# Attention inside a one-core diffusion step: key maxima beside the visits, and softmax sums without GpSimd

## The reference

```
keys = jnp.concatenate([_apply_rope(ak, cos, sin), cache['k']], axis=1)
vals = jnp.concatenate([av, cache['v']], axis=1)
...
s = jnp.einsum('bqkgd,bskd->bkgqs', qblk, k).astype(jnp.float32) * scale
p = jax.nn.softmax(s, axis=-1).astype(v.dtype)
return jnp.einsum('bkgqs,bskd->bqkgd', p, v)
```

## Time and profile before

| | us |
|---|---|
| median of 3 runs | 2387.59 (2383.01 to 2388.78) |
| the profiled execution, its own time | 2383.17 |
| its span, first to last instruction | 2381.4 |
| one steady attention tile (1216.14 to 1247.42) | 31.28 |
| the first attention tile (1156.38 to 1184.86) | 28.48 |
| the last one, to the next stage's first product (1372.62 to 1404.32) | 31.70 |

### The profile page before, as it was taken

How to read it: one execution, slowest core, us unless ns; L and a number is a source line. 1 busy time by engine, 2 the same in 40 slices (tenths; PEclk the granted TensorE clock), 3 DMA queues, 4 the chain that set the end, 5 groups by cost and what they waited for, 6 DMA issues and landing times. The chain is left out here.

```text
span 2381.4 us, 42995 instructions
## 1 busy us (share of the span) xinstructions
PE 2280.1 (96%) x17607; PEld 2024.0 (85%) x17607; DVE 1421.0 (60%) x2180; ACT 803.7 (34%) x1398; POOL 336.4 (14%) x291
## 2 busy tenths in 40 slices
PE   6999999999999999999888889998999999999997
PEld 5887779999999889998655569877999999998886
DVE  5331266533554566765666646768676676667877
ACT  5321132213333223324333444324223223234444
POOL 0000000001110001112466531000121121120001
PEclk9999999999999999999999989999999999999999
DMA  6325623235442533214101128421232232259434
GB/s 278 120 84 184 228 104 116 91 135 202 167 161 96 188 116 107 71 48 164 34 19 64 39 85 327 158 89 68 74 109 91 73 109 91 73 174 274 126 104 124
DMA packets 126875, 295.56 MB, mean 124 GB/s; under 512 B 19808, under 2 KB 63280, under 8 KB 117376
## 3 DMA queue, kind: packets, MB, share of 16 engines
q1 hardware_dynamic: 98112, 238.67, 29.8%
q10 hardware_dynamic: 24640, 39.46, 4.5%
q0 software_dynamic: 3968, 15.21, 1.7%
HBM read 207.83 MB, written 85.53 MB: 123 GB/s over the span
## 5 line engine op out<-in xcount | busy, mean ns | idle before, releaser
L62 PE MATMUL ps<-prj_w,h_hi 128*128 128x512 f32 (+1 forms) x864 | 254.9, 379 | 4.1 <-DVE h_lo L755 4.1
L62 PE MATMUL ps<-h_hi,fill_whi 128*128 128x384 f32 x672 | 235.2, 350 | 4.9 <-ACT fill_st L1119 2.4
L62 PE MATMUL ps<-wt 128*128 128x320 f32 (+2 forms) x1046 | 227.2, 327 | 2.3 <-DVE merged L3315 1.3
L62 PE MATMUL ps<-h_lo,fill_whi 128*128 128x384 f32 x672 | 226.1, 336 | 2.7 <-issue 2.7
L62 PE MATMUL ps<-h_hi,fill_wlo 128*128 128x384 f32 x672 | 226.5, 337 | 0.0
L62 PE MATMUL ps<-ys,mergedr 128*128 128x256 f32 (+1 forms) x1056 | 219.2, 296 | 0.4 <-issue 0.4
L62 PE MATMUL ps<-zb,mergedr 128*128 128x320 f32 (+2 forms) x764 | 200.4, 327 | 4.9 <-issue 2.7
L62 PE MATMUL ps<-zb,wt 128*128 128x384 f32 (+3 forms) x758 | 200.2, 325 | 0.0
L62 PEld LDWEIGHTS ps<-prj_w,h_hi 128*128 128x128 f32 x864 | 158.0, 190 | 42.7 <-issue 10.6
L62 PEld LDWEIGHTS ps<-wt 128*128 128x128 f32 x1046 | 179.6, 189 | 16.7 <-issue 2.6
L62 PEld LDWEIGHTS ps<-ys,mergedr 128*128 128x128 f32 x1056 | 174.2, 190 | 0.7 <-issue 0.7
(11 more groups left out here) (509 smaller groups left out, 4723.1 us busy)
## 6 DMA issues: line engine op xcount, KB each, us to landing
wraw<-in_w_ffn_in SPq DMA_DIRECT2D x22, 1024.0 KB, 5.2
prj_raw<-in_w_ada SPq DMA_DIRECT2D x16, 1024.0 KB, 5.8
fill_raw<-in_w_fill SPq DMA_DIRECT2D x30, 512.0 KB, 4.6
wtf<-a_dram SPq DMA_DIRECT2D x55, 256.0 KB, 2.6
bg_dram<-fill_st ACTq DMA_DIRECT2D x72, 192.0 KB, 2.0
xf<-bg_dram POOLq DMA_DIRECT2D x24, 576.0 KB, 7.1
tok_dram<-prj_tst ACTq DMA_DIRECT2D x45, 256.0 KB, 2.0
prj_raw<-in_w_tok SPq DMA_DIRECT2D x10, 1024.0 KB, 7.0
```

The lines of the kernel that those rows point to most:

```text
L62: mm = pe.matmul(out, lhs[a], rhs[b], start=first and n == 0, stop=last and n == 2, skip_group_check=onto)
```

## The change

Four edits of `attention`; nothing else is touched.

1. `shift` writes the maximum negated in one instruction, straight into `qpart`. The buffer `mx` and the semaphore `nm` are gone.
2. `add_trio` is gone. `sums(n)` multiplies each of the three tiles of a trio by ones: 24 products where there were 8 (the very last trio had 24 already). A ring slot is free when the trio's `sums` is done.
3. TensorE's order within a tile is new: two visits stand back to back and a head after them, `values` is followed at once by the same trio's `sums` (before, the third trio's `sums` fell into the next tile), `shifts(i, 1)` opens the tile, and `queries(i+2, 0)` is done at the end of tile i.
4. VectorE's `next_split(i+1, 1)` comes after head 0, `next_split(i+2, 0)` after head 6, `norm_b` after head 1. ScalarE's list and `turn` follow suit.

```diff
-        turn = lambda i, k: 4 * i + k + (1 if 4 * i + k >= 2 else 0)
+        def turn(i, k):
+            if i == 0:
+                return (0, 1, 3, 5)[k]
+            return 4 * i + (0, 2, 3, 5 if i < LAST else 4)[k]
...
             for i in range(LAST + 1):
-                if i:
-                    add_trio(3 * i - 1)
                 if i + 2 <= LAST:
                     rope(i + 2, 0)
-                add_trio(3 * i)
-                if i + 2 <= LAST:
                     rope(i + 2, 1)
-                add_trio(3 * i + 1)
...
+                if kv == 0 and i >= 3:
+                    pe.wait_ge(sem["norm"], i - 2)
                 turn_queries(pe, kv, PT).then_inc(sem["ptm"], 1)
...
             def shifts(i, kv):
-                pe.wait_ge(sem["nm"], AH * i + G * kv + G)
+                pe.wait_ge(sem["mx"], AH * i + G * kv + G)
                 pe.wait_ge(sem["pte"], turn(i, 2 + kv))
-                if kv == 1 and i >= 2:
+                if kv == 1 and i == LAST:
                     pe.wait_ge(sem["norm"], i - 1)
...
                 i, g = divmod(n, NT // TRIO)
                 if g == 0 and i:
                     pe.wait_ge(sem["rc"], i)
-                if n < LASTG:
-                    pe.wait_ge(sem["paired"], 2 * n + 2)
-                    mm = add(pt[(TRIO * n + TRIO - 1) % RING], g == 0, g == 2)
-                else:
-                    for x in range(TRIO):
-                        mm = add(pt[(TRIO * n + x) % RING], False, x == TRIO - 1)
+                for x in range(TRIO):
+                    mm = add(pt[(TRIO * n + x) % RING], g == 0 and x == 0, g == 2 and x == TRIO - 1)
...
+                shifts(i, 1)
+                head(0)
+                step(0)
+                step(1)
+                head(1)
+                if more:
+                    queries(i + 1, 1)
+                step(2)
+                step(3)
+                head(2)
+                values(i, 0)
+                sums(3 * i)
+                head(3)
+                step(4)
+                step(5)
+                head(4)
+                if more:
+                    shifts(i + 1, 0)
+                step(6)
+                head(5)
+                if i:
+                    spread_sums(i - 1)
+                values(i, 1)
+                sums(3 * i + 1)
+                head(6)
+                step(7)
+                step(8)
+                head(7)
+                if i + 2 <= LAST:
+                    queries(i + 2, 0)
+                values(i, 2)
+                sums(3 * i + 2)
...
-            shifts(0, 1)
+            queries(1, 0)
             for i in range(LAST + 1):
                 tile(i)
...
             def exponentials(i, j):
                 n = NT * i + j
-                b, r = divmod(n - RING, TRIO)
-                if b >= 0 and r < 2:
-                    act.wait_ge(sem["paired"], 2 * b + r + 1)
-                if b >= 0 and r == 2:
-                    act.wait_ge(sem["sums"], b + 1)
+                if n >= RING:
+                    act.wait_ge(sem["sums"], (n - RING) // TRIO + 1)
...
-            shifts(0, 1)
             put(23)
+            queries(1, 0)
...
-                v.tensor_reduce(mx[:, a % 2:a % 2 + 1], ps[:, 0:3, 0:TH], AX.XY, ALU.max).then_inc(sem["mx"], 1)
-                v.wait_ge(sem["mx"], AH * i + h + 1)
-                v.tensor_scalar(qpart[kv][:, a, 0:1], mx[:, a % 2:a % 2 + 1], -1.0, None, ALU.mult).then_inc(sem["nm"], 1)
+                v.tensor_reduce(qpart[kv][:, a, 0:1], ps[:, 0:3, 0:TH], AX.XY, ALU.max, negate=True).then_inc(sem["mx"], 1)
...
-                if 0 <= i < NT - 3:
-                    norm_b(i + 3)
                 for h in range(AH):
                     if i < LAST:
                         shift(i + 1, h)
+                    if 0 <= i < LAST and h == 0:
+                        next_split(i + 1, 1)
+                    if 0 <= i < NT - 3 and h == 1:
+                        norm_b(i + 3)
...
-                if i + 2 <= LAST:
-                    next_split(i + 2, 0)
-                    next_split(i + 2, 1)
+                    if i + 2 <= LAST and h == 6:
+                        next_split(i + 2, 0)
```

More of the change, by code:

```diff
@@ L1891, in attention @@
     RING, TRIO = 6, 3
-    LASTG = (LAT // P) * NT // TRIO - 1
     LAST = LAT // P - 1
@@ L1920, in attention @@
         prc = g.hole
-        mx = ph.sb("mx", [P, 2])
         ones, spread = ph.sb("ones", [P, 32]), ph.sb("spread", [P, G, HD])
@@ L1928, in attention @@
         names = ("load qload const knd kpow kout ktm kte qd qpow rope cpart qtm qte csmm cmx cex cptm cpte comm cdone "
-                 "part s1 mx nm ptm pte s2 ex pv paired sums rc spread norm evict yout0 yout1 kv dve mly mlw mlhi b0y1 b0y2 b0w b0yh b0wh b0yl b0wl b0mm b0ev b0out0 b0out1 b0out2 b0out3 b0out4 b0out5 b1lo")
+                 "part s1 mx ptm pte s2 ex pv sums rc spread norm evict yout0 yout1 kv dve mly mlw mlhi b0y1 b0y2 b0w b0yh b0wh b0yl b0wl b0mm b0ev b0out0 b0out1 b0out2 b0out3 b0out4 b0out5 b1lo")
         sem = {n: ph.sem(n) for n in names.split()}
@@ L2023, in rope @@
                 gp.wait_ge(sem["rope"], 6 * n + 3 * e + 3)
[L2025 to L2031, removed]
             inverse_norm(0)
@@ L2208, in spread_sums @@
                 if i < LAST:
-                    pe.wait_ge(sem["pte"], turn(i + 2, 2) + 1 if i + 2 <= LAST else turn(LAST, 3) + 1)
+                    pe.wait_ge(sem["pte"], (turn(i + 2, 2) if i + 2 <= LAST else turn(LAST, 3)) + 1)
                 else:
@@ L2220, in tile, with step, head @@
                 more = i < LAST
-                for j in range(NT):
+                def step(j):
                     for kv in range(KV):
                         scores(i, kv, j)
[L2224 to L2241, removed]
-                if more:
-                    shifts(i + 1, 1)
-                else:
-                    sums(LASTG)
+                def head(h):
+                    if more:
+                        shift_scores(i + 1, h)
+                shifts(i, 1)
[3 more added lines that the diff above has]
+                head(1)
+                if more:
+                    queries(i + 1, 1)
[24 more added lines that the diff above has]
+                sums(3 * i + 2)
             queries(0, 0)
@@ L2351, in tile @@
                 more = i < LAST
+                shifts(i, 1)
                 for j in range(NT):
                     exponentials(i, j)
-                    if more and j < 2:
-                        queries(i + 1, j)
+                    if more and j == 1:
+                        queries(i + 1, 1)
                     if more and j == 5:
```

## The result

| | before | after |
|---|---|---|
| median of 20 runs each, us | 2387.11 (2383.01 to 2389.36) | 2391.64 (2386.73 to 2395.67) |
| profiled execution, its own time | 2383.17 | 2395.01 |
| its span | 2381.4 | 2393.2 |
| start: `shifts(0, 0)` to `shifts(0, 1)` | 4.05 | 5.14 |
| tile 0 | 28.48 | 29.90 |

The ratio is 1.0019, with a 95% interval of 1.0012 to 1.0026. So the kernel after is slower by a little, and clear of the noise, though by less than the 0.3% that the forecast held to be the least that can be told. The forecast for the median was 2392.2. The four stretches of the two profiles differ by 1.09 + 1.42 + 0.44 + 2.56 = 5.5 us.

A forecast was written before the change was run, and what follows sets the result against it. TensorE's list, with its standing still between instructions, was taken to set the tile. Start +0.9, tile 0 +1.5, tiles 1 to 6 +1.3 and last tile +0.9 gave +4.6 us: 2387.6 + 4.6 = 2392.2, range 2382 to 2400.

The forecast's parts named there:

- Products: TensorE's sums: 24 products by ones take 1.44 us where 8 took 0.58; 2.6 us more per tile, all on the path.
- Walk of the steady tile: TensorE's starts followed from one `shifts(i, 1)` to the next: 31.57 us against 31.28, +0.3 per tile.
- wait for the reciprocal: A tile's first sums overwrite the bank VectorE's reciprocal reads, so TensorE newly stands 0.66 us, from 10.28 to 10.94.
- Pairs: Two visits back to back take 2.5 us against 1.88 of products; each loses 0.6 to ScalarE, four per tile.
- Stall at the split: Once per tile, the queries' turn waited 1.28 us for VectorE's split, 2.54 long beside a GpSimd addition; now gone.
- Negated maximum: Removing 64 VectorE instructions beneath heads' products gives nothing, except 0.2 in the first tile; a slower reduction costs 0 to +0.3 per tile.
- Start and tile 0: `shifts(0, 1)` comes near 1157.3 instead of 1156.38, +0.9 us; tile 0 takes 29.98 against 28.48, +1.5.
- Tiles 1 to 6: Six steady tiles at 0.29 us more each, less 0.4 since tile 6 has no queries to turn: +1.3.
- Last tile: Its sums grow to 3 × 1.44, +1.3 us, less 0.4 for one that ran at 1.2 GHz: +0.9.
- C: Rival, 4%: new gaps lower TensorE's clock in steady tiles, 14 us more, near 2406; other way, last tile keeps clock, 3 less.
- A: Rival, 23%: heads after pairs meet late maxima, or pairs cost 0.2 more each; 0.8 us more per tile, near 2398.
- D: Rival, 5%: TensorE's waits at pairs, reciprocal and head 5, with changes of shape, give −2 × 7 us: 2378.

## Why the prediction was right

The forecast was 2392.2, and 2391.64 was measured; as a difference, +4.6 was forecast, and +4.5 came between the medians and +5.5 in the stretches of the two profiles. Most of its terms hold. Two are mis-sized in opposite directions, −0.9 for tiles 1 to 6 and +1.7 for the last, and that they nearly cancel is luck.

**Products: right.** 1.44 per trio was forecast, 1.45 and 1.44 were measured, and the experiment that takes 16 of the 24 away gives back 0.89 each, on the path in full.

The Trainium skill (TensorE: Matmul & The Clock Gate, "Wait — 56ns, not 53.3ns?") states a floor of about 25 ns between starts of matmuls, however few columns they have. The trace is in line with it: the 0.89 us over the 32 records of a trio that this experiment leaves out is 28 ns each; no run here varies their columns. The Trainium skill's rule of up to four times the rate for products that narrow (TensorEngine Tiling (Array Packing), theoretical speedup) would have needed 15 ns and given 2383, and the sums of no run came near that.

**Walk of the steady tile: right to 0.13 us at its end, and to 0.3 at every step read.** Counted from the turn, TensorE starts `values` at 7.51 (forecast 7.58), sums at 10.70 (10.94), head 3 at 12.15 (12.38), the last sums at 30.00 (30.13) and the next turn at 31.44 (31.57). The wait for the reciprocal was forecast at 0.66, and 0.39 came: head 2 starts 0.09 earlier, and the reciprocal 1.27 after its reduction's start where the walk had 1.36. Pairs took 2.44, not 2.50. The queries' turn at the tile's end took 1252.54 − 1252.01 = 0.53, not 0.40, and gave part of it back.

**Stall at the split: right.** It is gone with the additions, and the old order with the additions left out shows that alone. The Trainium skill (SBUF — State Buffer, two separate sides) has VectorE and GpSimd hold one port pair in turn; the traces agree, with 427 ns at most in both kernels without additions against 2551 with them. The prediction's "no split can take more than its 0.43" leans on their places too: GpSimd still has its ropes, of 0.73 to 0.75 us each, and in the steady tile none of them runs beside a split. The kernel with the additions back shows that the place alone is enough (428 ns at most).

**Negated maximum: right.** Of its bound of 0 to 0.3 per tile, 0 came: 1358 ns as before, and alone it moved the time by a ratio of 0.9994.

**Start and tile 0: right.** +1.09 and +1.42, for +0.9 and +1.5.

**Tiles 1 to 6: mis-sized.** +1.3 was forecast, +0.44 came, from the 0.13 per tile above, which six tiles multiply. The prediction's account in words doesn't add up to its walk: about 5 gone and 2.6 + 2.4 + 0.66 new would be +0.7 per tile, not +0.3. The forecast rests on the walk.

**Last tile: mis-sized.** +0.9 was forecast, +2.56 came. The sums grew as forecast, 0.4 off included: by starts they took 1.01 (in the slow piece), 0.58 and 1.88 before, 3 × 1.45 after, which is +0.88. What failed is that all else in the tile was taken as unchanged. The prediction knew of one slow piece of 6.9 us; there were two, 10.3 us in all, and in the new order they are 14.0. The same `values` take 0.9 us more in them, and the visit of 1400.17 takes 2.00 us to the next instruction where the one of 1390.10 took 1.25. The sign was in the trace: "is never the late one" was read off ScalarE's own waits, and in the last tile before TensorE's visits wait for it 3.4 us in 6 places. The size is that of one pair of profiles; the kernel with the earlier reciprocal has the same last tile on TensorE and took 33.6, at a mean clock of 0.85 instead of 0.80.

The clock stood among the rivals (C), for the steady tiles, where it did not come. Its other direction, "if the last tile kept its clock, 3 us less", is borne out by the 3.6 us of the `values` and the spread; with the gaps filled as well it was 6.9.

**The other rivals.** A (late maxima or dearer pairs) did not come: the heads' weight loads wait 3.9 us in the whole stage. D (gaps that shrink) came at 0.13 per tile only, by itself; by hand the same gaps are fillable, as the kernels with sums in them show.

What stays open: what exactly in a last tile's gaps brings the clock down, and why the slow stretches are longer in the new order. In the profiles of the six kernels without products in those gaps the last tile had a granted clock of 0.80 to 0.89, in the one with them in two gaps 0.89, in the four with them in four gaps 1.00. The products both shorten the gaps and put records in them, and no run tells the two apart.

## What to carry to other kernels

Before work goes from an engine with time to spare to the one that sets the pace, look for what it really holds up: here the additions on GpSimd cost some 1.4 us per tile, through one split on VectorE, and with the splits elsewhere they stretch nothing that a steady tile waits for, while the products that replaced them cost 2.6. When an order must hold two steps back to back that wait on another engine, put small pieces of the pacing engine's own work between them: 0.57 us of products cost 0.23 there. Give a tail that lacks its usual filler an order of its own, and read its granted clock.

## What the hardware showed beyond that

- **Short gaps, none above 1.6 us, stood before stretches at half clock, and products put into them kept the clock full.** In the last tile of the kernel after, TensorE's visits wait for ScalarE 3.2 us in 5 places that the waits show, 1.6 at the longest, and still two stretches of 7.0 us ran at the 1.2 GHz level. With pieces of 16 records in the gaps the granted clock was 1.00 in four kernels of four, and the tile took 27.3 us. The waits that were left there are 0.5 us at the longest.
- **The runs' times go with the clock they are granted.** Of the 20 runs of the kernel after, the four with a mean granted clock of 0.991 took 2386.73 to 2389.35 us, and the six at 0.986 or 0.987 took 2391.34 to 2395.67. So two runs of one kernel can differ by 0.1% and more with no change at all; a stretch of the trace at one clock is the safer measure. Whether the clock is the whole of that difference these runs don't show.
